# Neighbourhood attention: six units' probabilities turned by VectorE and DRAM, relation table copies moved to the feed-forward stages

## The reference

```python
def _na_mixer(h, hc, w_in, rpb, w_out, need_ctx_out):
    q, k, v, g = jnp.split(h @ w_in, 4, axis=-1)
    kc, vc = jnp.split(hc @ w_in[:, WIDTH:3 * WIDTH], 2, axis=-1)
    ...
    s_loc = s_loc + bias[None]
    s_ctx = jnp.einsum('brqhd,bchd->bhrqc', q, kc).astype(jnp.float32)
    logits = jnp.concatenate([s_loc.reshape(b_, N_HEADS, rows, GRID_W, n_loc), s_ctx], axis=-1)
    p = jax.nn.softmax(logits, axis=-1).astype(v.dtype)
    ...
    o = jnp.einsum('bhrqik,brikhd->brqhd', p_blk, vb) + jnp.einsum('bhrqc,bchd->brqhd', p_ctx, vc)
    y = (o.reshape(b_, l_, WIDTH) * jax.nn.silu(g)) @ w_out
```

## Time and profile before

| | |
|---|---|
| median of 3 runs | 1814.83 us (1814.77 to 1815.89) |
| the profiled execution's own time | 1815.61 us |
| its span, first to last instruction | 1813.8 us |
| PE, PEld busy | 1793.3 us (99%), 1477.5 us (81%) |
| DVE, ACT, POOL busy | 954.2, 901.5, 1366.0 us |
| the 16 rounds and what belongs to them | about 304 to 386 us of the span |
| mean rate of the transfers | 206 GB/s |

### The profile page before, as it was taken

How to read it: one execution, slowest core, us unless ns; L and a number is a source line. 1 busy time by engine, 2 the same in 40 slices (tenths; PEclk the granted TensorE clock), 3 DMA queues, 4 the chain that set the end, 5 groups by cost and what they waited for, 6 DMA issues and landing times.

```text
span 1813.8 us, 24988 instructions
## 1 busy us (share of the span) xinstructions
PE 1793.3 (99%) x9274; PEld 1477.5 (81%) x9274; DVE 954.2 (53%) x1756; ACT 901.5 (50%) x1329; POOL 1366.0 (75%) x568
## 2 busy tenths in 40 slices
PE   6999999999999999999999999999999999999999
PEld 5888888887889888887788888888888878888887
DVE  4673766778755524866653230713095876143152
ACT  3324424674455644456554644464445565555452
POOL 2624544559968898977689798969897867888885
PEclk9999999999999999999999999999999999999999
DMA  9863885749775775565665566567655666656663
GB/s 366 291 210 94 270 310 163 198 141 312 244 277 200 211 221 191 180 198 168 209 186 192 179 195 191 193 187 234 191 193 185 192 190 182 196 160 210 190 195 128
DMA packets 206457, 372.91 MB, mean 206 GB/s; under 512 B 33508, under 2 KB 59092, under 8 KB 205780
## 3 DMA queue, kind: packets, MB, share of 16 engines
q1 hardware_dynamic: 203328, 363.69, 63.5%
q10 hardware_dynamic: 3028, 7.86, 1.2%
HBM read 367.27 MB, written 9.28 MB: 208 GB/s over the span
## 4 chain that ended last, share of the span: by engine, by line
PE 97%; DVE 2%; DMA 0%; issue 0%; ACTq 0%; ACT 0%; POOL 0%; DVEq 0%
PE ps L1300 26%; PE ps L1302 25%; PE ps L1301 25%; PE ps L1426 3%; PE ps L1427 3%; PE ps L1428 3%; PE ps L1992 1%; PE ps L1993 1%; PE ps L1994 1%; PE ps L1348 1%; PE ps L1697 1%; PE ps L1918 1%; PE ps L1668 1%; PE ps L1678 1%; PE ps L1962 1%; PE ps L1558 1%
## 5 line engine op out<-in xcount | busy, mean ns | idle before, releaser
L659 POOL TENSOR_TENSOR w_lo<-raw,w_hi 128x1024 fp32r<-128x1024 f32 x556 | 1347.1, 2461 | 397.4 <-ACT w_hi L697 376.2
L1300 PE MATMUL ps<-w_hi,act_rows_r 128*128 128x512 f32 x2064 | 814.8, 395 | 3.2 <-POOL w_lo L659 3.1
L1302 PE MATMUL ps<-w_hi,act_rows_r 128*128 128x512 f32 x2064 | 805.2, 390 | 0.0
L1301 PE MATMUL ps<-w_lo,act_rows_r 128*128 128x512 f32 x2064 | 804.6, 390 | 0.0
L697 ACT ACTIVATE w_hi<-raw 128x1024 fp32r<-128x1024 f32 x556 | 571.1, 1058 | 371.0 <-DMA raw<-in_ffn_w_up 100.8
L1300 PEld LDWEIGHTS ps<-w_hi,act_rows_r 128*128 128x128 f32 x2064 | 388.2, 188 | 90.4 <-issue 9.1
L1302 PEld LDWEIGHTS ps<-w_hi,act_rows_r 128*128 128x128 f32 x2064 | 388.0, 188 | 82.0
L1301 PEld LDWEIGHTS ps<-w_lo,act_rows_r 128*128 128x128 f32 x2064 | 388.4, 188 | 77.7
L2647 DVE STREAM_TRANSPOSE ps<-proj 32x256 f32<-32x256 f32 (+1 forms) x384 | 166.5, 434 | 6.5
L2628 DVE TENSOR_TENSOR proj<-proj,ps 128x1024 f32<-128x1024 f32 (+1 forms) x18 | 20.4, 1132 | 252.2 <-PE ps L1302 247.9
L1426 PE MATMUL ps<-act_rows_r,w_hi 128*128 128x512 f32 (+1 forms) x288 | 101.3, 352 | 0.0
(11 more groups left out here) (245 smaller groups left out, 1554.0 us busy)
## 6 DMA issues: line engine op xcount, KB each, us to landing
raw<-in_w_in SPq DMA_DIRECT2D x120, 512.0 KB, 3.9
raw<-in_ffn_w_gate SPq DMA_DIRECT2D x88, 512.0 KB, 4.4
raw<-in_ffn_w_up SPq DMA_DIRECT2D x88, 512.0 KB, 4.4
raw<-in_ffn_w_down SPq DMA_DIRECT2D x88, 512.0 KB, 4.2
proj<-in_ada_w SPq DMA_DIRECT2D x39, 512.0 KB, 7.9
pt<-in_ada_w SPq DMA_DIRECT2D x38, 512.0 KB, 6.4
raw<-in_pool_w_in SPq DMA_DIRECT2D x32, 512.0 KB, 7.3
raw<-in_na_w_in SPq DMA_DIRECT2D x32, 512.0 KB, 4.9
```

Of the source, the lines that this page charges most:

```text
L659: pool.tensor_tensor(w_lo[:, s, :], raw[:, s, :], w_hi[:, s, :].bitcast(F32), ALU.subtract).then_inc(lo_done, 1)
L1300: pe.matmul(o, h, hi, start=start, stop=False)
L1301: pe.matmul(o, h, lo, start=False, stop=False)
L1302: return pe.matmul(o, c, hi, start=False, stop=stop)
```

## The change

Units 0, 2, 4, 6, 8 and 10 (NA_SQUARED) are no longer turned by TensorE. VectorE transposes their probabilities in squares of 32x32 into a scratch place of the buffer bias (one instruction of 128x1024, in the place of its copy to pt); ScalarE issues one transfer of 512 KB to DRAM in the round after (keep_squares), and in the next round four transfers of 128 KB each that bring them back as blocks (place_squares). TensorE multiplies them with the values two rounds later than before, in round u + 5 and not u + 3, reading blocks in pieces of 32 with a step of 256. There is one scratch place and one place in DRAM: a store waits until the unit before has been brought back, and the transpose waits for the store before. The product of unit 10 gets bank 3. The other ten units go as before. keep_rel(l) moves behind the first eight weight groups of the feed-forward stage of its own layer.

```diff
+NA_SQUARED = (0, 2, 4, 6, 8, 10)
...
         def na_out_bank(u):
-            return 2 if u < NA_UNITS - 3 else 4
+            return 3 if u == NA_SQUARED[-1] else 2 if u < NA_UNITS - 3 else 4
+        def na_due(i):
+            return [u for u in range(NA_UNITS - 1) if u + (5 if u in NA_SQUARED else 3) == i]
...
-                if j in (1, 3):
-                    keep_rel(j // 2)
+            sp.wait_ge(na_kept, 16 * len(NA_SQUARED))
...
+                        if tables and pair == 0:
+                            keep_rel(l)
...
+                def keep_squares(u):
+                    act.wait_ge(dve_done, dve_s.count(("na_sq", u)))
+                    if u:
+                        act.wait_ge(na_placed, 64 * (u // 2))
+                    act.dma_start(na_squares[:], bias[:, 2048:3072]).then_inc(na_kept, 16)
+                def place_squares(u):
+                    act.wait_ge(na_kept, 16 * (u // 2 + 1))
+                    if u:
+                        act.wait_ge(pe_done, pe_s.count(("na_out", u - 2)))
+                    for kq in range(4):
+                        act.dma_start(na_placed_rows([[256, 4], [1, 256]], 0, slice(32 * kq, 32 * kq + 32)),
+                                      bass.AP(na_squares.tensor, 256 * kq, [[1024, 32], [32 * 1024, 4], [1, 256]])).then_inc(na_placed, 16)
...
-                        if i >= 3:
+                        if i - 3 in NA_SQUARED:
+                            act.wait_ge(dve_done, dve_s.count(("na_sq", i - 3)))
+                        elif i >= 3:
                             act.wait_ge(pe_done, pe_s.count(("na_t", i - 3, 1)))
...
+                    if i - 3 in NA_SQUARED:
+                        keep_squares(i - 3)
+                    if i - 4 in NA_SQUARED:
+                        place_squares(i - 4)
...
-                        act.wait_ge(pe_done, pe_s.count(("na_t", u, 1)))
-                        if u >= 2:
-                            act.wait_ge(pe_done, pe_s.count(("na_out", u - 2)))
-                        act.activation(pt[:, (u % 2) * 1024 + 512:(u % 2) * 1024 + 1024], ps[:, 7, :],
+                        if u not in NA_SQUARED:
+                            act.wait_ge(pe_done, pe_s.count(("na_t", u, 1)))
+                            if u >= 2:
+                                act.wait_ge(pe_done, pe_s.count(("na_out", u - 2)))
+                            act.activation(pt[:, (u % 2) * 1024 + 512:(u % 2) * 1024 + 1024], ps[:, 7, :],
...
+                if u in NA_SQUARED:
+                    pe.wait_ge(na_placed, 64 * (u // 2 + 1))
+                else:
...
+                        maps = na_placed_rows([[256, 4], [1, 32]], 32 * (4 * c + k)) if u in NA_SQUARED else pt[:, o:o + P]
...
-                    if i >= 2:
+                    due = na_due(i)
+                    for u in due[:-1]:
+                        na_values(u)
+                    if i >= 2 and i - 2 not in NA_SQUARED:
                         na_turned(i - 2)
-                    if i >= 3:
-                        na_values(i - 3)
+                    for u in due[-1:]:
+                        na_values(u)
...
+                    if u in NA_SQUARED:
+                        dve.wait_ge(act_done, act_s.count(("na_e", u, 1)))
+                        if u:
+                            dve.wait_ge(na_kept, 16 * (u // 2))
+                        dve.transpose(free(bias[:, 0:1], [[32, 8], [256, 4], [1, 32]], 2048),
+                                      na_rows_of(u, [[P, 8], [32, 4], [1, 32]])).then_inc(dve_done, dve_s.one(("na_sq", u)))
```

More of the change, by code:

```diff
@@ L174, in program @@
     map_rows = nc.dram_tensor("map_rows", (2, P, 768), F32, kind="Internal").ap()
+    na_squares = nc.dram_tensor("na_squares", (P, 1024), F32, kind="Internal").ap()
     gate_scratch = nc.dram_tensor("gate_scratch", (DEPTH, KC, 2, P), F32, kind="Internal").ap()
@@ L235, in program @@
         decay_in = sem("decay_in")
+        na_kept, na_placed = sem("na_kept"), sem("na_placed")
         maps_kept, maps_in = ([sem(f"{n}{k}") for k in range(2)] for n in ("maps_kept", "maps_in"))
@@ L304, in na_out_bank, with na_last_of, na_placed_rows @@
         def na_out_bank(u):
-            return 2 if u < NA_UNITS - 3 else 4
+            return 3 if u == NA_SQUARED[-1] else 2 if u < NA_UNITS - 3 else 4
+        def na_due(i):
+            return [u for u in range(NA_UNITS - 1) if u + (5 if u in NA_SQUARED else 3) == i]
+        def na_last_of(k):
+            return 4 * k + 2 if 4 * k + 2 in NA_SQUARED else 4 * k + 3
+        def na_placed_rows(dims, at=0, rows=slice(0, P)):
+            return free(proj[rows, 0:1], dims, CTX_RES + D + at)
         def na_rows_of(u, dims, at=0):
@@ L962, in na_layer @@
                         u = i - 2
-                        act.wait_ge(pe_done, pe_s.count(("na_t", u, 1)))
-                        if u >= 2:
-                            act.wait_ge(pe_done, pe_s.count(("na_out", u - 2)))
-                        act.activation(pt[:, (u % 2) * 1024 + 512:(u % 2) * 1024 + 1024], ps[:, 7, :],
-                                       ACT.Copy).then_inc(act_done, act_s.one(("na_pt", u, 1)))
+                        if u not in NA_SQUARED:
[3 more added lines that the diff above has]
+                            act.activation(pt[:, (u % 2) * 1024 + 512:(u % 2) * 1024 + 1024], ps[:, 7, :],
+                                           ACT.Copy).then_inc(act_done, act_s.one(("na_pt", u, 1)))
                         if i == NA_UNITS:
@@ L1682, in na_values @@
             def na_values(u):
-                pe.wait_ge(dve_done, dve_s.count(("na_pt", u, 0)))
-                pe.wait_ge(act_done, act_s.count(("na_pt", u, 1)))
+                if u in NA_SQUARED:
+                    pe.wait_ge(na_placed, 64 * (u // 2 + 1))
+                else:
+                    pe.wait_ge(dve_done, dve_s.count(("na_pt", u, 0)))
+                    pe.wait_ge(act_done, act_s.count(("na_pt", u, 1)))
                 bank = na_out_bank(u)
@@ L1696, in na_values @@
                         o = (u % 2) * 1024 + c * 512 + k * P
-                        last = pe.matmul(ps[c * HD:(c + 1) * HD, bank, 0:P], v, pt[:, o:o + P], start=k == 0, stop=k == 3)
+                        maps = na_placed_rows([[256, 4], [1, 32]], 32 * (4 * c + k)) if u in NA_SQUARED else pt[:, o:o + P]
+                        last = pe.matmul(ps[c * HD:(c + 1) * HD, bank, 0:P], v, maps, start=k == 0, stop=k == 3)
                 last.then_inc(pe_done, pe_s.one(("na_out", u)))
@@ L2438, in turned @@
                 def turned(u):
-                    dve.wait_ge(pe_done, pe_s.count(("na_t", u, 0)))
-                    if u >= 2:
-                        dve.wait_ge(pe_done, pe_s.count(("na_out", u - 2)))
-                    dve.tensor_copy(pt[:, (u % 2) * 1024:(u % 2) * 1024 + 512], ps[:, 6, :]).then_inc(dve_done, dve_s.one(("na_pt", u, 0)))
+                    if u in NA_SQUARED:
[4 more added lines that the diff above has]
+                                      na_rows_of(u, [[P, 8], [32, 4], [1, 32]])).then_inc(dve_done, dve_s.one(("na_sq", u)))
+                    else:
+                        dve.wait_ge(pe_done, pe_s.count(("na_t", u, 0)))
+                        if u >= 2:
+                            dve.wait_ge(pe_done, pe_s.count(("na_out", u - 2)))
+                        dve.tensor_copy(pt[:, (u % 2) * 1024:(u % 2) * 1024 + 512], ps[:, 6, :]).then_inc(dve_done, dve_s.one(("na_pt", u, 0)))
                     dve.wait_ge(act_done, act_s.count(("na_e", u, 1)))
@@ L2476, in gated @@
                     dve.wait_ge(pe_done, pe_s.count(("tp", "nag", 0, k)))
-                    dve.wait_ge(dve_done, dve_s.count(("na_o", 4 * k + 3)))
+                    dve.wait_ge(dve_done, dve_s.count(("na_o", na_last_of(k))))
                     z = ps[:, NA_Z_BANK[k], :].rearrange("p (c n) -> p c n", c=2)
@@ L2490, in na_layer @@
                         dve.wait_ge(pe_done, pe_s.count(("na_s", i)))
-                        if i >= 3:
+                        if i >= 3 and i - 3 not in NA_SQUARED:
                             dve.wait_ge(pe_done, pe_s.count(("na_t", i - 3, 1)))
@@ L2504, in na_layer @@
                         gated(0)
+                    due = na_due(i)
+                    for u in due[:-1]:
+                        values(u)
                     if i >= 2:
@@ L2508, in na_layer @@
                         gate_made(7)
-                    if i >= 3:
-                        values(i - 3)
+                    for u in due[-1:]:
+                        values(u)
                     if i == NA_UNITS // 2 - 1:
```

3 lines of the change are left out of this document (1 added, 2 removed).

## The result

The changed kernel takes 1829.38 us (median of 6 runs, 1825.86 to 1837.18) against 1814.80 for the kernel before on the same chip: ratio 1.0084, 95% interval [1.0067, 1.0102]. It is slower by 0.8%, well outside what I had called no change and outside my range. The profiled execution took 1830.02 us, its span 1828.2.

What follows compares the result with a forecast made beforehand. TensorE, without a gap in the neighbourhood attention rounds, was taken as the bound. 5.5 us saved less 0.3, 1.0, 0.2, 2.5 and 0.5 left 1.0 us: 1813.8 us, eight in ten 1810.2 to 1818.5.

Steps and rivals of the forecast that it cites:

- The wait that is added: Squares' trip through DRAM with one place: a turn taken as 7.5 us, just hidden in a 7.9 us pair of rounds.
- the 0.11: Chance of the rival that the trip through DRAM is the bound: 1818.8 us at 9.0 us a turn, 1821.3 at 9.5.
- The position tables: Tables for na_l of units 4 to 14 (even): 0.5 us of loss over six tables, range 0 to 5.
- the two rivals: Trip through DRAM as bound (0.11) and position tables as bound (0.07); they come together if both queues share 16 engines.
- the ring: Store, return, product and next store through one place; must turn once per pair of rounds, 7.9 us; taken as 7.5.
- ScalarE's queue: Transfer issues ahead of ScalarE's copies, 0.44 us each, counted at nothing; with no overlap 1.3 us beyond a pair of rounds.
- rival 0.07: Position tables are the bound, sharing transfer engines with the squares: six tables 1 us late, 1819.3 us; chance 0.07.
- The relation copies: Moved to the feed-forward stages, they cost nothing; rival that they aren't hidden: 2 us each, 1817.8 us, chance 0.03.
- What goes: Six units lose their TensorE transposes: 5.5 us saved, less 0.3 for values read in pieces of 32; left 5.2.
- The first rounds: Round 4 starts about 316.65 with unit 0's values still to do, so unit 0 wins nothing: 1.0 us lost.
- The last rounds: Rounds 14 to 16: unit 12's copies wait for unit 10's product and hold up later work; 2.5 us lost (1.5 to 3.5).
- The sum: 5.5 - 0.3 - 1.0 - 0.2 - 2.5 - 0.5 = 1.0 us faster, 1813.8 us; own case's chance 0.60.

Runs made afterwards that it cites:

- e3: Changed kernel without the six loads of position tables for units 4 to 15 (output not the reference's): 1821.84 us, ratio 1.0034 to the kernel before.
- e12: Changed kernel with the two relation table copies put back among the attention's tables and weight groups: 1840.29 us, ratio 1.0133 to the kernel before.
- e2: Changed kernel with two places in DRAM and two for the returned blocks: 1825.54 us, ratio 1.0064 to the kernel before.
- e5: Changed kernel, only units 0, 2, 4, 6, 8 squared, two places, product in round u + 7, unit 12's copies not waiting for a squared unit: 1818.44 us.
- e8: e5 without the position tables of units 4 to 15 (output not the reference's): 1811.97 us, ratio 0.9981 to the kernel before.
- e1: Kernel before with only the relation copies moved to the feed-forward stages: 1814.81 us, ratio 0.9996.
- e13: e5 with a third place for position tables and the products of units 0, 2, 4 and 6 in bank 3: 1813.06 us, ratio 0.9991.
- e14: e13 without unit 0, so only units 2, 4, 6 and 8 by squares: 1812.54 us, ratio 0.9983 to the kernel before.
- e4: Changed kernel, but unit 12's copies to pt wait for the last product that read their half (unit 8), not unit 10: 1825.50 us, ratio 1.0054.

## Why the prediction was wrong

**The step that failed** is "The wait that is added": "The row nearest in kind is the map, ... so I take 7.5: just hidden", with bounds 6.8 and 9.5. It measured 10.7, above the upper bound. The mechanism was named, and its formula as a rival comes near: 1814.8 - 1.5 + 5 x (10.7 - 7.9) = 1827.3 against 1829.4. (Its 14.0 us of idle were 11.8; the lower clock, which it didn't have, makes up for that.) What was wrong is the term and so the 0.11. What made it small:

- The map's row was for 384 KB. A third more of its 6.2 us is 8.3, which doesn't fit 7.9 any more. I took 6.8 for a lower bound and 7.5 for the value, and no row stands behind either. No run changes the size alone, but e3, without tables, turned in 8.6.
- The position tables got 0.7 us (7.5 for 6.8); e3 shows up to 2.1 us per turn, and 7.5 us of the whole time at the medians. The return is where it shows: 6.8 us from its first issue to the next store, where the map's took 3.6 to land, while the store, 3.9, is off by less. e12 shows that another neighbour can cost more.
- The upper bound was built from the 4.1 us of a weight group before the change. That row was measured without the squares in its way; with them it is 5.5. A price read from the neighbours of a new transfer is itself changed by it, so it was no upper bound.
- The DMA share did not warn of it. It is 0.84 in the earlier trace rows, but the map's row had been taken at 0.66 (store) and 0.87 (return), with weight groups on its queue. The stretch of its store and that of its return, before:

```profile
862.90:865.50 2.60, 2.60 (x13) 2.11 (x12) 2.54 (x8) 0.02 (x1) 2.60 (x2) 1.00 0.66 190
865.50:869.60 4.10, 4.10 (x23) 2.98 (x22) 2.15 (x7) 3.74 (x10) 2.25 (x2) 1.00 0.87 248
```

- The sentence by the Trainium skill's rule (DMA: Bandwidth & Descriptors, "Issuing engines are not separate DMA queues") that transfers from SyncE and ScalarE run on the same 16 engines and interleave was right to tie the two rivals together. e3 agrees with it: the returns, issued by ScalarE, land in 2.7 us without SyncE's tables and in 3.6 with them. I gave both rivals together 0.18.

The estimate by the Trainium skill (DMA: Bandwidth & Descriptors, "Anatomy of one DMA") stands in a section on transfers that GpSimd issues, and these came from ScalarE. Its 3.2 us for a store is the median that the stores took to land; its 7.5 for the ring is not borne out, 10.7 was measured, and 8.6 without tables.

**What the ring hid.** Even with no ring (e2), one unit's way through DRAM was longer than the 9.1 us it had. I worked out the turn and not the way, so I had no term for what e2 shows: it gained only 4 us.

**ScalarE's queue** I counted at nothing for its issues, since its sequencer works ahead. That holds where the store has landed early: at 340.65 the issues ran beside the exponentials and nothing stood idle behind them. Where it lands late, ScalarE computes nothing during the issues, 2.76 us at 331.28. In e5 that is behind 1.54 us of TensorE's time; in the change TensorE waits for the squares then anyway. The 7.0 of 7.9 us that I gave as ScalarE's use was also misread: 13.94 of 20 us is 5.5 of 7.9.

**The lower clock** was in no step: about 3 us, shown by the rows at 0.50. The waits for the squares are up to 3.3 us long, and two of the five went with half the clock.

**The position tables** I put at 0.5 us, rival 0.07. In the change TensorE never waits for one, while its rounds are longer than before; VectorE does (1.95 us at 329.25). In e5, with the ring out of the way, two late tables cost TensorE 3.3 us, and without tables (e8) the time falls by 6.5. That the rival said 6 is luck: it had six tables 1 us late each. So the tables were second in the queue, and the chance of "tables or ring" was what mattered.

**The relation copies** at nothing: right (e1). That they would cost about 10 us if they stayed beside the squares I had not seen (e12).

**What goes**, 5.5 - 0.3: right. The even rounds take 3.51 us for the 3.5 given, VectorE's transpose of 128x1024 1.25 us for 1.3, and a product in pieces of 32 takes 1.03 us from its start to the next scores (326.90 - 325.87) where a plain one takes 1.02, so the 0.3 was not there.

**The first rounds**, 1.0 us: right in kind. Scores of round 4 start at 317.23 after 0.48 us of idle time; set back by the 0.41 us by which round 0 started later, that is 316.8 for the 316.65 given. That unit 0 brings nothing is what e13 and e14 say.

**The last rounds**, 2.5 us: right. Turn of the gate 1.52 us late (1.5 given), transposes of unit 13 0.95 (0.8 given), the out projection 389.35 - 376.26 = 13.1 us after the scores of round 15 (about 13 given), and e4 gives back 3.9 us at the medians (over runs that spread by 11 us in the change and by 5 in e4).

**The sum.** Without the 11.8 us of idle and the 3 at half clock the change would have taken about 1814.6 us, within 0.2% of before (estimate from its own rows; no run has all six units and no wait). e14 keeps four of the savings, has 0.6 us of waits, and wins 2.5 us.

## What to carry to other kernels

A trip through DRAM is a latency and a share of the same transfer engines. Price it from a row of the same size taken beside the same neighbours. If there is none, scale the row in full and set the upper bound well above it: a similar DMA share was no guard here. Then ask two questions, whether a turn fits its period and whether one unit's way fits its delay. More places alone gained 4 us (e2); more places with a later product, one unit fewer and e4's wait gained 11 (e5). When one wait of a shared resource goes, look for the next user of that resource: squares, then tables, then a bank.

## What the runs showed of the hardware

- Copies that cost nothing in one neighbourhood (ratio 0.9996 [0.9987, 1.0005], e1) cost about 10 us in another (e12 against the change, 11 at the medians, 9 by the ratios), with no change of their own.
- Position tables in pieces of 1 KB were not measurably better for the transfers beside them than in pieces of 256 bytes (1829.2 and 1829.4 us, over runs that spread by 7 and 11 us).
- With idle times of TensorE of 3.34 and 2.71 us (the change) and of 1.80 (e5) the granted clock went to 0.50 for some 3 us each; with others of 2.91 (the change) and 2.42 (e2) it did not. It was already down (0.76 on average in 336.5 to 337) before the first of them ended, and in the second it fell only about 1.5 us after TensorE had resumed (0.90 in 370.5 to 371).
- Four issues of a return took 1.8 to 2.8 us on ScalarE's queue, where I had counted 4 x 0.44 = 1.8. At 331.28, the longest, the engine's next work began only behind them.
